# The experts' up products in wide form from the third slot on, their sums dealt among the steps of the route choice

## The chip, the core and the metric

One program runs on one core of a Trainium2 chip. The metric is the device time of one execution in microseconds (us). A core has TensorE (PE, with its weight loads shown apart as PEld), VectorE (DVE), ScalarE (ACT), GpSimd (POOL) and SyncE (SP, which here only issues transfers). The engines run side by side, each works through its own list in order, and they meet on semaphores.

## What is computed

The reference runs two transformer blocks over 256 tokens of width 1024. The change lies in the last layer of the second block, a PEER layer with 16384 experts:

```python
s1, i1 = lax.top_k(s[:, :, 0], PEER_TOPK)
s2, i2 = lax.top_k(s[:, :, 1], PEER_TOPK)
cand_s = (s1[..., :, None] + s2[..., None, :]).reshape(T, PEER_HEADS, PEER_TOPK * PEER_TOPK)
top_s, pos = lax.top_k(cand_s, PEER_TOPK)
experts = jnp.take_along_axis(cand_i, pos, axis=-1)
g = jax.nn.softmax(top_s, axis=-1).astype(xb.dtype)
act = jax.nn.gelu(jnp.einsum('td,thkd->thk', xb, u)) * g
return jnp.einsum('thk,thkd->td', act, v)
```

Each token picks 16 experts per head by two rounds of top-16 (the route choice); its output is the gated sum of those experts. Every number is fp32.

## The kernel before

The kernel does not gather rows of the expert tables. It computes gelu(u·x) for all 16384 experts, multiplies it by a gate that is zero for experts not chosen, and multiplies by the whole second table. So both tables, 64 slots of 1 MB each, stream through the core once.

**The weight stream.** SP loads the stream in halves of 512 KB (128 partitions of 1024 fp32) into a ring of 6 places (line 1398). A place is loaded again when TensorE has finished with its last content (semaphore half_multiplied). ScalarE rounds each half to the part `ring_hi` (line 1856, `split`), and GpSimd subtracts to get the rest `ring_lo` (line 1413). The operand x has been split likewise into `h_hi` and `h_lo`, which lie side by side as `h_both`. A product in fp32 quality is hi·hi + hi·lo + lo·hi.

**Narrow up products** (`channels`, called by `experts(s)`, slots 0 to 24 of the up table). For each of 8 steps over the width and each half, three matmuls of 256 columns add to one bank: `ring_hi` on `h_hi`, `ring_hi` on `h_lo`, `ring_lo` on `h_hi`: 48 matmuls in a slot. Slots use three banks in turn. ScalarE's part (`activations`, line 892) is: split two halves, wait for the slot's product, apply gelu from the bank to `H`.

**Wide up products** (`wide_product`, called by `wide_experts(s)`, slots 25 to 62). `ring_hi` is multiplied on both parts of x in one matmul of 512 columns, then `ring_lo` on `h_hi` with 256: 32 matmuls in a slot. The product hi·lo lands in the second 256 columns of each bank, so somebody must add it. ScalarE copies that half of the bank to `H` (line 926), VectorE adds it to the first half in place (`columns`, line 1258), and ScalarE applies gelu one slot later (line 923). A slot takes two banks, and slots alternate between banks 0, 1 and 2, 3: TensorE may start slot s only when gelu of slot s-2 is done (h_ready). ScalarE's list for a wide slot s (`low_products`) is: split half 2s+4 of the up table; wait for the sum of slot s-1; split half 2s+5; gelu of slot s-1; wait for TensorE's slot s; copy its low products.

**The route choice on VectorE.** For each block of 128 tokens `best` runs rounds of 8 largest values, their indices and their replacement over 16 groups of 128 and then 8 groups of 256. Then come two casts (1227, 1228), four rounds of compare, multiply and reduce (1233, 1237, 1238), and a softmax whose exponential is ScalarE's (line 905, with the waits routes_shifted before and routes_exp after). TensorE transposes the result (585 to 587), ScalarE and VectorE copy it to `ROUTE` and the lookup area. VectorE has no part in the narrow slots, so the choice has it for itself; its sums begin with slot 25. After slot 31 the gates join: one-hot products per 8 tokens between the slots.

**The order** is written out by hand for each engine; there is no planner. Loops (`Fori`) stand for slots 5 to 22 on TensorE.

Of the kernel before, what the change touches and what calls it, by code (L numbers as in the profile page):

```python
# [5 lines left out]
SEQ = 256  # L6
D = 1024
TOK = 2
# [46 lines left out]
def build(nc, dram):  # L55
# [8 lines left out]
    with ctx:  # L64
# [231 lines left out]
        FIRST_WIDE = 25  # L296
# [51 lines left out]
        def pe_second(pe, weights, weights_ready, multiplied, parts, norm_transposes, wait_operand, wait_normed, token_product, out_product):  # L348
# [240 lines left out]
            last.then_inc(S["routes_transposed"], 1)  # L589
# [121 lines left out]
        def act_second(act, split, ahead, round_to, load_roots, root, norm_act):  # L711
# [186 lines left out]
            for s in range(2, 5):  # L898
                activations(s)
            with act.Fori(0, 5) as it:  # L900
                for s in range(5, 8):
                    activations(s, it)

            act.wait_ge(S["routes_shifted"], 1)
            A.activation(TV, TV, ACT.Exp).then_inc(S["routes_exp"], 1)
            act.wait_ge(S["x_stored"], 32)
            for s in range(20, 23):
                activations(s)
            act.wait_ge(S["routes_transposed"], 1)
            A.copy(ROUTE[:, 0:2, :].rearrange("p s t -> p (s t)"), ps[:, 4, :]).then_inc(S["routes_copied"], 1)  # L910

            A.mul(ROUTE[:, 2, :], ps[:, 5, 0:256], GATE_SCALE).then_inc(S["routes_copied"], 1)
            for s in range(23, FIRST_WIDE):
                activations(s)
# [13 lines left out]
            for s in range(FIRST_WIDE, 33):  # L928
                low_products(s)
# [49 lines left out]
        def dve_second(dve, step, inverse, wait_rounded, rest_of, norm_dve):  # L979
# [219 lines left out]
            def best(rows, values, indices, low=-3e38):  # L1199

                for first in (0, 8):
                    for r, v, i in zip(rows, values, indices):
                        last = V.max(v[:, first:first + 8], r)
                    step(last)
                    for r, v, i in zip(rows, values, indices):
                        last = V.max_index(i[:, first:first + 8], v[:, first:first + 8], r)
                    step(last)
                    if first == 0:
                        for r, v, i in zip(rows, values, indices):
                            last = V.match_replace(r, v[:, 0:8], r, low)  # L1210
                        step(last)

            for t in range(TOK):
                dve.wait_ge(S["sim_copied"], t + 1)
                g = range(16)
                best([SC[:, t, n, :] for n in g], [T1V[:, t, n, :] for n in g], [T1I[:, t, n, :] for n in g])
# [5 lines left out]
                best([CS[:, t, n, :] for n in g], [TV[:, 8 * t + n, :] for n in g], [TP[:, 8 * t + n, :] for n in g])  # L1222
# [4 lines left out]
            step(V.tensor_copy(PA, PAI))  # L1227
            step(V.tensor_copy(T1F, T1I))
            dve.wait_ge(S["sk_loaded"], 32)
            for t in range(TOK):  # L1230
                for side in range(2):
                    place = PA[:, side, t * 128:(t + 1) * 128].unsqueeze(2).broadcast_to([128, 128, 16])
                    step(V.tensor_tensor(EQ.rearrange("p (g a) -> p g a", a=16), place,
                                         iota[:, 0:16].unsqueeze(1).broadcast_to([128, 128, 16]), ALU.is_equal))
                    eq = EQ.rearrange("p (h k a) -> p h k a", h=8, k=16)
# [1324 lines left out]
```

## Time and profile before

| | us |
|---|---|
| median of 3 runs | 1524.72 (1524.34 to 1526.68) |
| the profiled execution | 1527.34 |
| its span in the trace | 1525.4 |
| TensorE busy in the span | 1496.1 (98%) |
| VectorE, ScalarE, GpSimd busy | 957.5, 807.1, 1190.6 |

The up slots 2 to 24 run from 775 to 908 us of the span, the first wide slots (25 to 31) from 908 to 948, and the slots with gates from there. The route choice fills VectorE from 768 to 886. An entry of the timeline is: start, duration, engine, line, operation, output and inputs; brackets give how long the engine had been idle and what released it. Matmuls overlap, so the pace of TensorE is read from start to start, not from durations.

### The profile page before, as it was taken

How to read it: one execution, taken by the hardware profiler on the slowest of the kernel's cores; microseconds unless marked ns; L12 is line 12 of the kernel's file. 1: busy time of each engine (PE TensorE's matmuls, PEld its weight loads, DVE VectorE, ACT ScalarE, POOL GpSimd, SP SyncE). 2: the span in 40 equal slices, each digit the busy share in tenths (PEclk: the TensorE clock that was granted, in tenths of full speed). 3: DMA queues.
4: the chain of work that ended last, by engine and by line, in shares of the span. 5: the costliest groups of instructions: out<-in, count | busy, mean ns of one | idle time of the engine just before them, and what ended most of it. 6: DMA issues, size and time to landing. Idle time of an engine off the chain costs nothing.

```text
span 1525.4 us, 28491 instructions
## 1 busy us (share of the span) xinstructions
PE 1496.1 (98%) x10230; PEld 1305.8 (86%) x10230; DVE 957.5 (63%) x1382; ACT 807.1 (53%) x1091; POOL 1190.6 (78%) x501
## 2 busy tenths in 40 slices
PE   6999999999999999999999999999999999999998
PEld 5698888887899989998899998888888778788886
DVE  6654665565432578542589922877779999944444
ACT  4566655557564565545554455555554444444443
POOL 6745688885888866498978998777777777789995
PEclk9999999999999999999999999999999999999999
DMA  8624565565655543356645555555555555566663
GB/s 291 235 94 143 169 192 185 188 191 158 189 180 164 167 140 114 109 196 213 214 152 181 180 180 178 170 172 167 167 173 171 166 174 171 176 224 196 190 194 119
DMA packets 72487, 268.17 MB, mean 176 GB/s; under 512 B 8144, under 2 KB 8416, under 8 KB 71008
## 3 DMA queue, kind: packets, MB, share of 16 engines
q1 hardware_dynamic: 69696, 251.90, 52.1%
q0 software_dynamic: 1856, 9.49, 1.6%
q10 hardware_dynamic: 864, 5.77, 1.0%
q8 instruction: 53, 0.87, 0.2%
q14 instruction: 18, 0.15, 0.0%
HBM read 263.98 MB, written 3.15 MB: 175 GB/s over the span
## 4 chain that ended last, share of the span: by engine, by line
PE 59%; POOL 18%; issue 15%; DVE 5%; ACT 1%; DMA 1%; DVEq 0%; POOLq 0%; ACTq 0%; SPq 0%
PE ps L1339 58%; POOL ring_lo L1413 17%; DVE onehots_i L1267 1%; DVE h_both L2114 1%; DVE big L1286 1%; DMA ring<-in_stream 1%; DVE onehot_j L1271 1%; ACT ring_hi L1856 1%; DMA big<-in_filt 0%; DVE big L2140 0%; DVE big L2142 0%; DVE big L2139 0%; DVE h_both L2131 0%; PE ps L1588 0%; PE ps L1488 0%
## 5 line engine op out<-in xcount | busy, mean ns | idle before, releaser
L1413 POOL TENSOR_TENSOR ring_lo<-ring,ring_hi 128x1024 fp32r<-128x1024 f32 x472 | 1167.8, 2489 | 311.5 <-ACT ring_hi L1856 309.2
L1856 ACT CAST ring_hi<-ring 128x1024 fp32r<-128x1024 f32 x472 | 491.8, 1051 | 436.5 <-DMA ring<-in_stream 433.7
L1339 PE MATMUL ps<-h_both,ring_hi 128*128 128x256 f32 (+1 forms) x2816 | 703.4, 330 | 2.1 <-DVE h_both L2131 1.8
L1339 PE MATMUL ps<-h_both,ring_lo 128*128 128x256 f32 x1952 | 549.8, 282 | 0.0
L1339 PEld LDWEIGHTS ps<-h_both,ring_hi 128*128 128x128 f32 x2816 | 473.6, 190 | 54.6 <-issue 3.1
L1339 PE MATMUL ps<-ring_hi,h_both 128*128 128x512 f32 (+1 forms) x1408 | 428.9, 382 | 9.0 <-POOL ring_lo L1413 5.2
L1339 PEld LDWEIGHTS ps<-h_both,ring_lo 128*128 128x128 f32 x1952 | 371.1, 190 | 0.4
L1339 PEld LDWEIGHTS ps<-ring_hi,h_both 128*128 128x128 f32 x1408 | 259.8, 188 | 64.9 <-issue 11.0
L1339 PE MATMUL ps<-ring_lo,h_both 128*128 128x512 f32 (+1 forms) x704 | 265.5, 377 | 0.0
L2114 DVE TENSOR_TENSOR h_both<-big,h_both 128x512 fp32r<-128x512 f32 (+1 forms) x66 | 138.0, 2091 | 99.8 <-ACT h_both L1869 99.7
L1339 PEld LDWEIGHTS ps<-ring_lo,h_both 128*128 128x128 f32 x704 | 132.7, 188 | 22.6
L1339 PE MATMUL ps<-big 128*64 128x64 f32 (+11 forms) x980 | 98.7, 289 | 10.4 <-DMA big<-in_filt 8.2
L1339 PEld LDWEIGHTS ps<-big 128*64 128x64 f32 (+4 forms) x980 | 74.9, 163 | 27.8 <-issue 15.8
L1286 DVE TENSOR_TENSOR big<-ps,big 128x512 f32 (+1 forms) x64 | 86.0, 1344 | 1.5 <-ACT big L923 1.1
L1267 DVE TENSOR_TENSOR onehots_i<-routes,ps 128x1024 f16<-128x1024 f32 (+1 forms) x64 | 77.5, 1211 | 0.0
L1258 DVE TENSOR_TENSOR ps<-ps,big 128x512 f32<-128x512 f32 x38 | 26.6, 699 | 75.9 <-ACT big L926 75.9
L2376 DVE SCALAR_TENSOR_TENSOR big<-ps,vecs,big 128x255 f32<-128x255 f32 (+1 forms) x88 | 36.4, 475 | 25.8 <-ACT big L2068 25.8
L1339 PE MATMUL ps<-q_both,ring_hi 128*128 128x512 f32 x128 | 45.0, 396 | 0.0
L2381 DVE TENSOR_TENSOR ps<-big 128x256 f32<-128x256 f32 x22 | 42.3, 1923 | 3.4 <-ACT big L2044 1.2
L1869 ACT ACTIVATE h_both<-big 128x512 fp32r (+2 forms) x66 | 42.1, 640 | 3.4 <-DVE big L1286 3.3
L1271 DVE TENSOR_TENSOR onehot_j<-routes,ps 128x512 f16<-128x512 f32 (+1 forms) x64 | 43.4, 678 | 0.0
L1275 DVE TENSOR_TENSOR onehots_j_even<-onehot_j,ps 128x1024 f16<-128x1024 f16 x32 | 39.1, 1221 | 4.4
(325 smaller groups left out, 1459.6 us busy)
## 6 DMA issues: line engine op xcount, KB each, us to landing
ring<-in_stream SPq DMA_DIRECT2D x476, 512.0 KB, 3.8
big<-in_cmp_values POOLq DMA_DIRECT2D x2, 1024.0 KB, 11.5
residual<-big ACTq DMA_DIRECT2D x2, 1024.0 KB, 4.8
big<-residual ACTq DMA_DIRECT2D x2, 1024.0 KB, 6.6
x<-in_x SPq DMA_DIRECT2D x2, 512.0 KB, 5.4
big<-in_fdecay POOLq DMA_DIRECT2D x1, 1024.0 KB, 8.9
aux<-in_tab POOLq DMA_DIRECT2D x1, 1024.0 KB, 11.9
big<-in_w POOLq DMA_DIRECT2D x1, 1024.0 KB, 15.1
```

The source lines that it names most:

```text
L1258: V.tensor_tensor(sums, sums, H[:, bass.ds(at(2 * s, 12, it), 2), :], ALU.add).then_inc(S["columns_summed"], 1)
L1267: V.tensor_tensor(OA[:, q % 2], first.unsqueeze(2).broadcast_to([128, 8, 128]), IOTA.unsqueeze(1).broadcast_to([128, 8, 128]), ALU.is_equal)
L1271: V.tensor_tensor(ONEHOT_J[:, :, :], second.unsqueeze(2).broadcast_to([128, 8, 64]), IOTA[:, 64 * half:64 * half + 64].unsqueeze(1).broadc ...
L1275: V.tensor_tensor(OB[q % 2][:, :, :, :], ONEHOT_J[:, :, :].unsqueeze(1).broadcast_to([128, 2, 8, 64]), GATE_PARTS[:, :, bass.ds(tok, 8)].u ...
L1286: V.tensor_tensor(h, ps[:, bank, :].rearrange("p (t j) -> p t j", t=8), h, ALU.mult).then_inc(S["gated"], 1)
L1339: return nc.tensor.matmul(out, lhsT, rhs, start=start, stop=stop, skip_group_check=True)
L1413: P.tensor_tensor(ring_lo[:, h % RING, :], ring[:, h % RING, :], ring_hi[:, h % RING, :].bitcast(fp32), ALU.subtract).then_inc(S["split_lo ...
L1856: A.copy(ring_hi[:, h % RING, :], ring[:, h % RING, :]).then_inc(S["split_hi"], 1)
L1869: A.activation(dst, src, ACT.Copy, scale=scale).then_inc(S["operand_hi"], 1)
L2114: V.tensor_tensor(lo, src, hi.bitcast(fp32), ALU.subtract).then_inc(S["operand_lo"], 1)
L2376: V.scalar_tensor_tensor(y, ffn_place(i, j)[:, 0:SEQ - s], vecs[:, bass.ds(col, 1)], y, ALU.mult, ALU.add).then_inc(S["ffn_tap"] if tap el ...
L2381: V.tensor_tensor(gated, CONV[:, i % 2, 0, :], CONV[:, i % 2, 1, :], ALU.mult).then_inc(S["ffn_product"], 1)
```

## The change

`FIRST_WIDE` goes from 25 to 2: slots 2 to 24 take the wide form too, with all that belongs to it on ScalarE and VectorE. VectorE's 23 new sums of these slots are put between the steps of the route choice by hand (`columns_after`), and 3 more (25 to 27) after it. TensorE's transposes of the routes move from behind slot 22 to behind slot 27. On ScalarE the exponential moves from in front of slot 20 to behind the low products of slot 25, and the copies of the routes to behind those of slot 27.

```diff
-        FIRST_WIDE = 25
+        FIRST_WIDE = 2
@@ TensorE
-            for s in range(2, 5):
-                experts(s)
-            with pe.Fori(0, 6) as it:
-                for s in range(5, 8):
-                    experts(s, it)
+            for s in range(FIRST_WIDE, 5):
+                wide_experts(s)
+            with pe.Fori(0, 3) as it:
+                for s in range(5, 11):
+                    wide_experts(s, it)
+            for s in range(23, 28):
+                wide_experts(s)
...
-            for s in range(23, FIRST_WIDE):
-                experts(s)
-            for s in range(FIRST_WIDE, 32):
+            for s in range(28, 32):
                 wide_experts(s)
@@ ScalarE
+            for s in range(FIRST_WIDE, 5):
+                low_products(s)
+            with act.Fori(0, 3) as it:
+                for s in range(5, 11):
+                    low_products(s, it)
+            act.wait_ge(S["x_stored"], 32)
+            for s in range(23, 26):
+                low_products(s)
+            act.wait_ge(S["routes_shifted"], 1)
+            A.activation(TV, TV, ACT.Exp).then_inc(S["routes_exp"], 1)
+            for s in range(26, 28):
+                low_products(s)
+            act.wait_ge(S["routes_transposed"], 1)
+            A.copy(ROUTE[:, 0:2, :].rearrange("p s t -> p (s t)"), ps[:, 4, :]).then_inc(S["routes_copied"], 1)
+            A.mul(ROUTE[:, 2, :], ps[:, 5, 0:256], GATE_SCALE).then_inc(S["routes_copied"], 1)
+            for s in range(28, 33):
                 low_products(s)
@@ VectorE
                     for r, v, i in zip(rows, values, indices):
                         last = V.max(v[:, first:first + 8], r)
                     step(last)
+                    if ("max", first) in columns_after:
+                        next_columns()
...
+                     (("max", 8), ("index", 8)) + ((("index", 0), "replace") if t else ()))
...
+                     (("max", 0), "replace", ("max", 8)) if t else (("max", 0), ("index", 0), ("max", 8), ("index", 8)))
...
             step(V.tensor_copy(PA, PAI))
+            next_columns()
             step(V.tensor_copy(T1F, T1I))
+            next_columns()
...
                     step(V.tensor_tensor(EQ.rearrange("p (g a) -> p g a", a=16), place,
                                          iota[:, 0:16].unsqueeze(1).broadcast_to([128, 128, 16]), ALU.is_equal))
+                    next_columns()
...
                     step(V.tensor_reduce(IX[:, side, t, :], EQ.rearrange("p (g a) -> p g a", a=16), AX, ALU.add))
+                    next_columns()
...
             V.tensor_tensor(TV, TV, wide(inv), ALU.mult).then_inc(S["routes_ready"], 1)
+            for s in range(summed[0], 28):
+                columns(s)
```

## Rows read from the trace of the kernel before

**Rows 1.** The page, part 1: engine, busy us and share, count.

```profile
PE 1496.1 (98%) x10230; PEld 1305.8 (86%) x10230; DVE 957.5 (63%) x1382; ACT 807.1 (53%) x1091; POOL 1190.6 (78%) x501
```

**Rows 2.** The chain that ended last, 740 to 960 us: start, us, what.

```profile
739.78 156.24 PE ps L1339 x1264
...
936.79 4.43 DMA ring<-in_stream
...
942.89 17.17 PE ps L1339 x121
```

**Rows 3.** PE's timeline: narrow steps, the first wide slot, a query step.

```profile
907.90 0.28 PE L1339 MATMUL ps<-h_both,ring_lo 128*128 128x256 f32 x1
908.02 0.40 PE L1339 MATMUL ps<-h_both,ring_hi 128*128 128x512 f32 x1
...
911.91 0.40 PE L1339 MATMUL ps<-h_both,ring_hi 128*128 128x512 f32 x1
...
724.71 0.40 PE L1339 MATMUL ps<-q_both,ring_hi 128*128 128x512 f32 x1
...
730.95 0.40 PE L1339 MATMUL ps<-q_both,ring_hi 128*128 128x512 f32 x1
```

**Rows 4.** ACT's timeline beside narrow slots: gelu (L892), two splits (L1856).

```profile
792.38 0.60 ACT L892 ACTIVATE big<-ps 128x512 f32<-128x512 f32 x1 [0.96 <-PE ps L1339]
...
796.70 1.05 ACT L1856 CAST ring_hi<-ring 128x1024 fp32r<-128x1024 f32 x1 [2.09 <-DMA ring<-in_stream]
...
867.36 0.60 ACT L892 ACTIVATE big<-ps 128x512 f32 x1 [0.87 <-PE ps L1339]
...
870.90 1.05 ACT L1856 CAST ring_hi<-ring 128x1024 fp32r<-128x1024 f32 x1 [1.52 <-DMA ring<-in_stream]
```

**Rows 5.** ACT's timeline beside wide slots: copy (L926), splits, gelu (L923).

```profile
930.80 0.59 ACT L926 COPY big<-ps 128x512 f32<-128x512 f32 x1 [0.15 <-PE ps L1339]
...
935.25 1.05 ACT L1856 CAST ring_hi<-ring 128x1024 fp32r<-128x1024 f32 x1 [2.02 <-DMA ring<-in_stream]
936.21 0.59 ACT L923 ACTIVATE big<-ps 128x512 f32<-128x512 f32 x1
```

**Rows 6.** PE's timeline at a wide slot's start: idle before, releaser.

```profile
936.34 0.28 PE L1339 MATMUL ps<-h_both,ring_lo 128*128 128x256 f32 x1
936.85 0.50 PE L1339 MATMUL ps<-h_both,ring_hi 128*128 128x512 f32 x1 [0.23 <-ACT big L923]
```

**Rows 7.** DVE's timeline: the sum of a wide slot.

```profile
931.42 0.70 DVE L1258 TENSOR_TENSOR ps<-ps,big 128x512 f32<-128x512 f32 x1 [4.92 <-ACT big L926]
```

**Rows 8.** DVE's timeline: first operation of steps of the route choice.

```profile
767.79 3.19 DVE L1203 MAX8 aux<-big 128x8 f32<-128x128 f32 x16 [10.01 <-ACT big L882]
771.01 0.09 DVE L1206 MATCH_VALUE_LOAD aux<-aux,big 128x8 f32 x1
...
775.32 0.09 DVE L1210 MATCH_VALUE_LOAD big<-aux,big 128x8 f32 x1
...
855.98 4.47 DVE L1233 TENSOR_TENSOR ps<-aux 128x2048 f32<-128x2048 f32 x1
```

**Rows 9.** ACT's timeline about the exponential: table load and activation.

```profile
879.50 1.28 ACT L905 ACT_TABLE_LOAD   x1
884.11 0.42 ACT L905 ACTIVATE aux<-aux 128x256 f32<-128x256 f32 x1 [3.33 <-DVE aux L1243]
```

**Rows 10.** DVE's timeline behind the exponential.

```profile
884.56 0.42 DVE L1245 TENSOR_REDUCE stat<-aux 128x16 f32<-128x256 f32 x1 [0.49 <-ACT aux L905]
...
885.30 0.42 DVE L1247 TENSOR_TENSOR aux<-aux,stat 128x256 f32<-128x256 f32 x1
```

**Rows 11.** Busy time by stretch: engines in page order, clock, DMA share, GB/s.

```profile
775.00:896.00 121.00, 121.00 (x1011) 121.00 (x1010) 108.90 (x362) 60.42 (x66) 107.74 (x41) 1.00 0.56 177
```

**Rows 12.** GpSimd's group of 849 to 884 us, and of 885 to 907.

```profile
L1413 POOL TENSOR_TENSOR ring_lo<-ring,ring_hi 128x1024 fp32r<-128x1024 f32 x11 | 34.3, 3155 | 0.4 <-ACT ring_hi L1856 0.4
...
L1413 POOL TENSOR_TENSOR ring_lo<-ring,ring_hi 128x1024 fp32r<-128x1024 f32 x9 | 21.4, 2404 | 2.2 <-ACT ring_hi L1856 2.2
```

More of the change, by code:

```diff
@@ L897, in act_second @@
                 similarities(t)
[L898 to L914, printed above, removed]
             def low_products(s, it=None):
@@ L926, in low_products @@
                 A.copy(H[:, bass.ds(at(2 * s, 12, it), 2), :], ps[:, wide_banks(s), SEQ:2 * SEQ]).then_inc(S["low_products_copied"], 1)
-            for s in range(FIRST_WIDE, 33):
+            for s in range(FIRST_WIDE, 5):
[14 more added lines that the diff above has]
+            for s in range(28, 33):
                 low_products(s)
@@ L1196, in dve_second, with columns, next_columns, best @@
                         rest_of(SCALED[:, c, :], h_hi[:, c, :], h_lo[:, c, :])
-            def best(rows, values, indices, low=-3e38):
+            def columns(s, it=None):
+                dve.wait_ge(S["low_products_copied"], at(EXPERT_SUMS + s - FIRST_WIDE + 1, 6, it))
+                sums = ps[:, wide_banks(s), 0:SEQ]
+                V.tensor_tensor(sums, sums, H[:, bass.ds(at(2 * s, 12, it), 2), :], ALU.add).then_inc(S["columns_summed"], 1)
+            summed = [FIRST_WIDE]
+            def next_columns():
+                columns(summed[0])
+                summed[0] += 1
+            def best(rows, values, indices, columns_after, low=-3e38):
                 for first in (0, 8):
@@ L1207, in best @@
                     step(last)
+                    if ("index", first) in columns_after:
+                        next_columns()
                     if first == 0:
@@ L1215, in dve_second @@
                 g = range(16)
-                best([SC[:, t, n, :] for n in g], [T1V[:, t, n, :] for n in g], [T1I[:, t, n, :] for n in g])
+                best([SC[:, t, n, :] for n in g], [T1V[:, t, n, :] for n in g], [T1I[:, t, n, :] for n in g],
+                     (("max", 8), ("index", 8)) + ((("index", 0), "replace") if t else ()))
                 halves = T1V[:, t].rearrange("p (h s) k -> p h s k", s=2)
@@ L1221, in dve_second @@
                 g = range(8)
-                best([CS[:, t, n, :] for n in g], [TV[:, 8 * t + n, :] for n in g], [TP[:, 8 * t + n, :] for n in g])
+                best([CS[:, t, n, :] for n in g], [TV[:, 8 * t + n, :] for n in g], [TP[:, 8 * t + n, :] for n in g],
+                     (("max", 0), "replace", ("max", 8)) if t else (("max", 0), ("index", 0), ("max", 8), ("index", 8)))
             tp = TP.rearrange("p g k -> p (g k)")
@@ L1252, in dve_second @@
             dve.wait_ge(S["gate_rest"], 1)
-            def columns(s, it=None):
-                dve.wait_ge(S["low_products_copied"], at(EXPERT_SUMS + s - FIRST_WIDE + 1, 6, it))
-                sums = ps[:, wide_banks(s), 0:SEQ]
-                V.tensor_tensor(sums, sums, H[:, bass.ds(at(2 * s, 12, it), 2), :], ALU.add).then_inc(S["columns_summed"], 1)
             def onehots(q, it=None):
@@ L1292, in rest @@
                 rest_of(flat(H[:, bass.ds(at(2 * s, 2 * span, it), 2), :]), flat(h_hi[:, place, :]), flat(h_lo[:, place, :]))
-            for s in range(FIRST_WIDE, 31):
+            for s in range(28, 31):
                 columns(s)
```

19 lines of the change are left out of this document (11 added, 8 removed).

## The prediction

> **What bounds the kernel now.** The page's first part gives TensorE 98% of the span [rows 1]. A share over the whole span says nothing of one stage, so the second view is the chain of waits over the stage that is changed. There the chain is TensorE's own matmuls without a break through the narrow slots and the first wide ones. But for the transposes of the routes it leaves TensorE only near 937 us, for a transfer of the ring, a split and TensorE again [rows 2]. The third view, busy time by stretch, says that from 775 to 896 us TensorE is busy all the time, VectorE 90%, GpSimd 89% and ScalarE 50%, at full clock [rows 11]. The stage costs what its matmuls cost, and a change shows in the time as far as TensorE's slots get shorter and nothing new holds them up. All that follows the stage hangs on the same chain, so a shift here should come through to the end.
>
> **Shorter slots.** The pace is read from start to start. Narrow: 907.90 to 908.02, so 0.12 us a matmul, and 48 of them make 5.76 [rows 3]. Wide, same operands: 908.02 to 911.91 is 11 steps of one 512 and one 256 columns, 0.3536 each, so 5.65 for 16 [rows 3]. The gain is 0.11 us in each of slots 2 to 24: 23 x 0.11 = 2.5 us off. The query products with the same shapes run faster: 724.71 to 730.95 is 18 steps, 0.3467 each, 5.55 a slot [rows 3], which would give 23 x 0.21 = 4.9. I take the first, since it has the same operand and stands next to the changed slots; the other is the bound. That the wide slot is the longer one I exclude, since these rows have it shorter at either pace.
>
> What the page of TensorE makes of this: the Trainium skill, "TensorE: Matmul & The Clock Gate", section "Back-to-back issue gap", gives an isolated matmul N/2.4 + 2.5 ns. By that the narrow step would be 3 x 109.2 = 327.5 ns and the wide one 215.8 + 109.2 = 325.0, an estimate of only 0.04 us a slot and 0.9 in all. The rows show 360 and 354 ns, so the trace does not agree in size.
>
> **The loop behind a wide slot.** What the wide form adds is a chain that the narrow one, with three banks, never had to meet. Slot s+2 needs gelu of slot s. Gelu of slot s stands on ScalarE behind the split of a half whose ring place is freed only when slot s ends. From the rows: copy of slot 28 at 930.80; its second split starts at 935.25, 4.45 later, released by the transfer; gelu at 936.21; TensorE starts slot 30 at 936.85, 1.60 after the split, having waited on that gelu [rows 5, 6]. The copy starts about 0.2 after TensorE's next slot has begun when nothing stalls, so slot s+2 may begin without loss until 5.65 - 0.2 = 5.45 after the copy. The transfer may therefore take 5.45 - 1.6 = 3.85 us from the copy to the split. In narrow slots the same distance is 3.54 (867.36 to 870.90) at best and 4.32 (792.38 to 796.70) at worst [rows 4]; these two are the ends of 21 such pairs, six of which exceed 3.85, by 0.9 us together. Of the wide slots 25 to 31 two lost 0.4 each: slot 30 could have begun 0.12 after 936.34 and began at 936.85, and slot 31 at 942.89 came 6.04 after it [rows 2, 6]. At the narrow pairs' rate 23 new slots lose about 1.0 us. If every fourth met the 4.45 of slot 28, 0.6 too much, they would lose 5.75 x 0.6 = 3.5; if every one did, half of it each, since a slot begun late gives the next one room: 6.9. The former has more samples, and I take it: +1.0, from 0 to 3.5.
>
> **The sums on VectorE.** A sum takes 0.70 and can begin 0.62 us after the copy of its low products starts (930.80 to 931.42) [rows 5, 7]. It costs nothing if done before ScalarE's second split, 3.8 us after the copy. VectorE reaches them between steps of the choice. A step of 16 maxima takes 3.2 us, one of 16 indices or replacements 4.3 [rows 8]; a compare takes up to 4.5. Between two sums there are two steps at most. Laying them out against slots of 5.65, VectorE is ahead and waits at slots 3, 5, 7, 10, 11, 12, and from 16 on at nearly each. The tightest is slot 8: from slot 7's sum, at which VectorE waited, 0.65 + 0.70 + 3.2 + 4.3 + 0.7 = 9.55 after the copy of slot 7, against 5.65 + 3.8 = 9.45. That is 0.1 late; with the next tight one, slot 13 (0.5 to spare), I take +0.2, from 0 to 1.5 if steps come out a few per cent longer. The choice, whose softmax began at 884.56 [rows 10], ends at about 907, since VectorE is now tied to TensorE's pace. TensorE wants the routes behind slot 27, about 923, and the gates' copies after slot 31, about 946, so that delay is hidden.
>
> **The exponential.** In the kernel before it cost TensorE nothing: three banks, and ScalarE waited for VectorE inside slack. Now it stands behind the low copy of slot 25, and the sum of slot 25 stands behind the softmax on VectorE. From that copy's start: copy 0.6, table load 1.28, exponential 0.42 [rows 9], VectorE's reduce to product 884.56 to 885.72, 1.2 [rows 10], sum 0.7: 4.2 us. Only then ScalarE may split the second half (not at 3.8), and ahead of gelu it must load gelu's table again, 1.28 [rows 9]: 4.25 + 1.6 + 1.3 = 7.15 after the copy, where 5.45 is free. Slot 27 is held up by +1.7 us. Without VectorE's part it would be 3.75 + 1.6 + 1.3 - 5.45 = 1.2, the lower bound; the upper is 2.5 with a late transfer. One slot later the loop has recovered: the place for the next split was freed in time, and slot 27 itself takes 5.65.
>
> **Costs at nothing.** GpSimd needs 2.4 us a half when alone and took 3.16 in the compare steps [rows 12]. Those steps cost it some 8 us beyond 11 x 2.4, whatever the pace; 46 halves x 2.4 plus that and 3 more for casts are 121 of 130 us. It can lag some 6 us before TensorE waits, since a half is needed 13.8 us after its place is freed and takes 3.8 + 1.05 + 2.4. The copies (0.6 a slot) fall on ScalarE's idle half. Six transposes move and cost the same 0.7. SP's queue keeps its order; its loads come 2% closer together. Slots 2 and 3 meet no wait, since gelu of slots 0 and 1 is long done.
>
> **Sum.** -2.5 + 1.0 + 0.2 + 1.7 = +0.4 us, on the profiled execution's 1527.34 (span 1525.4 and 1.9 around it). That execution lies 2.6 above the median of the runs, so I put the same +0.4 on the median: 1525.1.
>
> **The rivals.** *The query pace.* The new slots run at 5.55, the free time drops to 5.35, and stalls eat a little more (1.3): -4.9 + 1.3 + 0.2 + 1.7 = -1.7, 1523.0; with no stall on transfers and the short form of the exponential -3.7, 1521.0. For it: two measured levels and no row that names the cause; against it: all wide slots on `h_both` here stand at 5.65. Chance 0.22. *The transfer becomes the bound,* the case on the slow side: beyond 3.85 us between copy and split it costs time. With slot 28's 4.45 in every fourth slot: -2.5 + 3.5 + 0.2 + 1.7 = +2.9, 1527.6; with it in all, -2.5 + 6.9 + 1.9 = +6.3, 1531.0. For it: the only stretch of this form without gates ended in such stalls, and the chain shows it [rows 2]; against it: the distances of the narrow slots, whose transfers come only 2% less often [rows 4]. Chance 0.17. *VectorE late:* if the steps with interleaved sums run 5% longer, slots 4, 8, 9 and 13 come late by up to 0.5 each: +2.4, 1527.1. Chance 0.03. *The slot does not get shorter:* 5.76 as before, with room of 3.96 for the transfer: 0 + 0.5 + 0 + 1.6 = +2.1, 1526.8. It would do so if the 512 columns cost what two matmuls of 256 cost; the row at 908.02 speaks against it. The page named above comes near this, with 0.04 a slot. Chance 0.05. *The forecast,* between -2 and +2.5: 0.53.
>
> **How the numbers follow.** A run of this kernel can tell about 0.2%, 3 us, from no change. The forecast's case holds 0.47 of "same" and 0.03 on either side; the query pace 0.10 same and 0.12 faster; the transfer 0.05 same and 0.12 slower; the two small ones 0.05 same and 0.03 slower. Faster 0.15, same 0.67, slower 0.18. The range runs from the low end of the query pace, 1521.2, to 1529.0, well into the transfer's case, and leaves out about 1 in 8.
>
> **What would show it.** In the profile after: starts of slots 5.65 apart (step 0.354) in slots 3 to 24; TensorE idle 0.1 to 0.5 us before a few slots with gelu (the activation of `low_products`) as releaser; one stall of 1.7 before slot 27 with two table loads beside it; VectorE idle before most sums from slot 16 on; 23 more sums of 0.70 us. A step of 0.347 in those slots, distances from copy to split above 4 as a rule, or GpSimd as TensorE's releaser would make the prediction wrong.

## The result: slower by 0.3%

| | before | after |
|---|---|---|
| median in us (8 runs each) | 1526.66 (1524.34 to 1527.74) | 1531.48 (1527.87 to 1533.41) |
| the profiled execution, us | 1527.34 | 1528.75 |
| its span | 1525.4 | 1526.9 |
| slots 2 to 25, start to start | 133.2 | 133.3 |
| slots 25 to 31, start to start | 34.9 | 36.4 |

The ratio of the times is 1.0032 (95% interval 1.0021 to 1.0043). The last two rows of the table are read from the starts of the slots' first matmuls; the six transposes of the routes (0.66 us) lie in the first of them before and in the second after. The prediction was +0.4 us, so 1525.1, in a range from 1521.2 to 1529.0; the change costs 4.8 us here, and 1531.48 lies above the range. 2 us of the distance to 1525.1 are the kernel before itself, which measured 1526.66 in these runs and not 1524.72; even without them it would be 1529.5.

The page of the kernel after, part 1, answers [rows 1]:

```profile
PE 1494.1 (98%) x9862; PEld 1285.5 (84%) x9862; DVE 962.6 (63%) x1405; ACT 818.2 (54%) x1114; POOL 1187.3 (78%) x501
```

368 matmuls are gone (23 slots x 16), TensorE is busy 2 us less, and the span is 1.5 us longer: the work got shorter and the waits ate more than that. Busy time by stretch, 775 to 908 us, of the kernel after, with the columns of [rows 11]:

```profile
775.00:908.00 133.00, 131.39 (x736) 112.00 (x735) 112.07 (x375) 73.68 (x92) 117.09 (x46) 1.00 0.53 177
```

TensorE, which was busy without a break in the narrow slots [rows 11], now idles 1.6 us in this stretch alone, and GpSimd, at 117 of 133 us (88%, against 89% before), is no closer to being the bound. The chain that ended last shows where the breaks come from (start, us, what; kernel after). It answers [rows 2], but the pattern now stands in the choice's stretch:

```profile
739.94 51.59 PE ps L1358 x347
791.55 0.04 SPq L1417
791.69 3.95 DMA ring<-in_stream
795.72 0.09 ACT ring_hi L1875
...
796.68 0.59 ACT big L906
797.27 0.23 issue
797.50 23.18 PE ps L1358 x128
```

A ring place is freed at 791.55, the transfer takes 3.95 us, the split and gelu follow, and slot 6 begins only then. ScalarE's and TensorE's timelines at the same place (kernel after; L909 is the copy of low products, L1875 the split, L906 gelu) answer [rows 5] and [rows 6]:

```profile
791.56 0.59 ACT L909 COPY big<-ps 128x512 f32<-128x512 f32 x1 [0.52 <-PE ps L1358]
...
795.72 1.05 ACT L1875 CAST ring_hi<-ring 128x1024 fp32r<-128x1024 f32 x1 [1.83 <-DMA ring<-in_stream]
796.68 0.59 ACT L906 ACTIVATE big<-ps 128x512 f32 x1
```

```profile
797.50 0.47 PE L1358 MATMUL ps<-h_both,ring_hi 128*128 128x512 f32 x1 [0.34 <-ACT big L906]
```

From copy to second split it is 4.16 here, and from the split to TensorE's start 797.50 - 795.72 = 1.78. In the slots written out without a loop it had been 1.60 [rows 5, 6].

The stall before slot 27, from the same chain (L920 is the exponential and its table load, L1201 the sum of slot 25 behind the softmax, L906 gelu's table load):

```profile
913.56 0.59 ACT big L909
...
914.16 1.28 ACT L920
...
915.46 0.43 ACT aux L920
...
917.07 0.62 DVE ps L1201
...
917.72 1.05 ACT ring_hi L1875
...
918.79 1.28 ACT L906
...
920.73 5.92 PE ps L1358 x32
```

920.73 - 913.56 = 7.17 from the copy, where the prediction had 7.15.

### The profile page after: what moved, and what is told of

It is laid out like the page before. It is cut to its first block, busy times and chain, and to the rows that moved or that the text cites. A ratio compares the mean times of both kernels' runs of the same rounds, so it can differ in the third digit from the quotient of the medians.

```text
span 1526.9 us, 27863 instructions
## 1 busy us (share of the span) xinstructions
PE 1494.1 (98%) x9862; PEld 1285.5 (84%) x9862; DVE 962.6 (63%) x1405; ACT 818.2 (54%) x1114; POOL 1187.3 (78%) x501
## 4 chain that ended last, share of the span: by engine, by line
PE 59%; POOL 18%; issue 15%; DVE 3%; DMA 3%; ACT 2%; POOLq 0%; DVEq 0%; SPq 0%; ACTq 0%
PE ps L1358 58%; POOL ring_lo L1432 17%; DMA ring<-in_stream 2%; ACT ring_hi L1875 1%; DVE onehots_i L1286 1%; DMA big<-in_filt 0%; DVE h_both L2133 0%; ACT big L906 0%; DVE big L2159 0%; DVE big L2161 0%; DVE big L2158 0%; DVE onehot_j L1290 0%; DVE h_both L2150 0%; DVE big L1305 0%; PE ps L1607 0%
## 5 line engine op out<-in xcount | busy, mean ns | idle before, releaser
L1875 ACT CAST ring_hi<-ring 128x1024 fp32r<-128x1024 f32 x472 | 492.1, 1051 | 442.1 <-DMA ring<-in_stream 435.9
L1358 PE MATMUL ps<-h_both,ring_hi 128*128 128x512 f32 (+1 forms) x2448 | 699.8, 353 | 5.4 <-ACT big L906 3.1
L1358 PEld LDWEIGHTS ps<-h_both,ring_hi 128*128 128x128 f32 x2448 | 427.9, 189 | 76.4 <-issue 7.6
L1358 PEld LDWEIGHTS ps<-ring_lo,h_both 128*128 128x128 f32 x704 | 132.6, 188 | 22.5
L1201 DVE TENSOR_TENSOR ps<-ps,big 128x512 f32<-128x512 f32 x61 | 42.7, 699 | 78.7 <-ACT big L909 78.4
L909 ACT COPY big<-ps 128x512 f32 (+1 forms) x61 | 35.8, 587 | 40.4 <-PE ps L1358 40.2
L2395 DVE SCALAR_TENSOR_TENSOR big<-ps,vecs,big 128x255 f32<-128x255 f32 (+1 forms) x88 | 36.4, 475 | 25.6 <-ACT big L2087 25.6
```

Source lines behind the costliest of these rows:

```text
L909: A.copy(H[:, bass.ds(at(2 * s, 12, it), 2), :], ps[:, wide_banks(s), SEQ:2 * SEQ]).then_inc(S["low_products_copied"], 1)
L1201: V.tensor_tensor(sums, sums, H[:, bass.ds(at(2 * s, 12, it), 2), :], ALU.add).then_inc(S["columns_summed"], 1)
L1358: return nc.tensor.matmul(out, lhsT, rhs, start=start, stop=stop, skip_group_check=True)
L1875: A.copy(ring_hi[:, h % RING, :], ring[:, h % RING, :]).then_inc(S["split_hi"], 1)
L2395: V.scalar_tensor_tensor(y, ffn_place(i, j)[:, 0:SEQ - s], vecs[:, bass.ds(col, 1)], y, ALU.mult, ALU.add).then_inc(S["ffn_tap"] if tap el ...
```

## The experiments

A table of what the profiles show comes first, since the texts below use it. "2 to 25" and the others are distances between the starts of those slots; the ratio is to runs of the kernel before on the same chip. In the kernels whose name begins with "before" slots 2 to 24 are narrow. The six transposes (0.66) lie in 2 to 25 there, and in 25 to 31 elsewhere; in before_late_transposes they lie in 25 to 31 too.

| kernel | 2 to 25 | 25 to 31 | gated, 34 to 58 | ratio (95% interval) |
|---|---|---|---|---|
| before | 133.2 | 34.9 | 149.1 | |
| before_again | 133.2 | 34.4 | 149.1 | 1.0003 (0.9993 to 1.0013) |
| before_third | 133.2 | 34.3 | 146.8 | |
| after | 133.3 | 36.4 | 149.1 | 1.0032 (1.0021 to 1.0043) |
| after_again | 133.6 | 36.6 | 149.1 | 1.003 (1.002 to 1.004) |
| after_third | 132.8 | 36.8 | 149.1 | |
| exp_as_copy | 132.7 | 35.8 | 146.7 | 1.0016 (1.0005 to 1.0026) |
| unrolled | 133.5 | 37.0 | 149.1 | 1.0027 (1.0013 to 1.004) |
| unrolled_gelu_first | 127.7 | 35.2 | 146.7 | 0.9961 (0.9945 to 0.9976) |
| loops_gelu_first | 130.0 | 35.1 | 146.7 | 0.9969 (0.9957 to 0.9981) |
| exp_in_gap | 129.6 | 34.3 | 146.7 | 0.9962 (0.9948 to 0.9975) |
| sums_earlier | 129.7 | 34.3 | 146.7 | 0.9973 (0.996 to 0.9986) |
| sum_behind_pairs | 127.7 | 34.2 | 149.4 | 0.9959 (0.9944 to 0.9974) |
| before_gelu_first | 133.6 | 33.9 | 149.1 | 1.0011 (1.0002 to 1.002) |
| before_late_transposes | 133.1 | 34.3 | 146.7 | 0.9986 (0.9977 to 0.9995) |
| gelu_first_from_28 | 132.6 | 36.1 | 146.7 | 1.0018 (1.0007 to 1.0028) |

Three theories stood at the start. A: the loop from a freed place over transfer, split and gelu sets the start of a wide slot. B: VectorE's sums, squeezed between the steps of the choice, come late. D: something outside slots 2 to 31 differs from one execution to the next. A fourth, E, came up on the way.

### The changed kernel again

after_again, no edit.

> The changed kernel once more, unedited, for a second profile: its times fell into two groups, near 1528 (the profiled one) and near 1532. If the distance from the copy of low products to the second split sets the start of wide slots (theory A), the total of TensorE's idle time before the slots 2 to 31 accounts for all that one execution has over another: an execution of 1532 shows some 4 us more in starts of slots 4 to 31 than the 1528 one, and those slots show distances above 3.9. If something outside the stage varies (theory D), the starts of slots 2 to 31 are the same in both and the difference lies before 774 or behind 950 us. Median against before: 1.003.

Its median is 1527.75 on a chip where the kernel before has 1523.2, so the change costs about the same there, 4.6 us. Its profiled execution took 1527.61, 1.1 us less than the first one, and yet more in the stage: 170.3 us from slot 2 to 31 against 169.8. So what separates these two executions lies outside the stage, as theory D has it. No profile caught an execution near 1532, and what those do otherwise stays open.

The second profile also shows a wait that the first has not. ScalarE's second split behind the copy of slot 4 is released by VectorE's sum and not by the transfer (L909 copy, L1875 split, L1201 the sum):

```profile
792.40 0.58 ACT L909 COPY big<-ps 128x512 f32<-128x512 f32 x1 [0.51 <-PE ps L1358]
793.49 1.05 ACT L1875 CAST ring_hi<-ring 128x1024 fp32r<-128x1024 f32 x1 [0.51 <-DMA ring<-in_stream]
796.72 1.05 ACT L1875 CAST ring_hi<-ring 128x1024 fp32r<-128x1024 f32 x1 [2.17 <-DVE ps L1201]
```

TensorE idles 0.55 us before slot 6 for it. The third profile has the same wait, 4.27 us from copy to split. Theory B therefore holds for one slot in two of three profiles; TensorE's other waits for gelu between slots 4 and 25 stand behind a transfer.

### The exponential left out

```diff
-            A.activation(TV, TV, ACT.Exp).then_inc(S["routes_exp"], 1)
+            A.activation(TV, TV, ACT.Copy).then_inc(S["routes_exp"], 1)
```

> The exponential of the routes' softmax is left out (a copy stands in its place), so ScalarE loads no other table in the stage. All other waits stay. If the two table loads are what holds slot 27 (1.6 us in the profile of the changed kernel), slot 27 starts 5.7 after slot 26 and the time falls by 1.6 (ratio to before 1.002 instead of 1.003). If VectorE's place behind the softmax is what holds it, less than 0.4 us is gained.

The ratio fell from 1.003 to 1.0016, about 2 us (1.4 by the medians), with intervals that overlap. In the profile slot 27 started 6.34 after slot 26 and not 7.4: a transfer took 4.86 from copy to split just there, so a good part of the stall stayed under another name. Without the table loads the stall is smaller in this profile, which supports the step; the exact 1.6 isn't shown by this run. Its gated slots ran 2.4 us faster (34 to 58), which was not expected and could by itself account for the gain in the median. It is what led to the last theory below.

### Without the loops

```diff
-            with pe.Fori(0, 3) as it:
-                for s in range(5, 11):
-                    wide_experts(s, it)
+            for s in range(5, 23):
+                wide_experts(s)
```

and the same for `low_products` on ScalarE.

> Slots 5 to 22 written out without the loops on TensorE and ScalarE, same order. In the changed kernel's loops TensorE starts a slot 1.78 after the second split, against 1.60 in the slots written out. Theory A: that 0.18 falls on most of 18 slots, so the mean start-to-start there goes from 5.80 to 5.68 and the time falls by about 2 us, somewhat less as stalls share. Theory B (VectorE's sums come late): no change in the mean, 5.80. If the instruction fetch of the longer programs disturbs the transfers, it gets slower instead, with more distances above 4.2.

The expected 2 us did not come: the ratio stayed at 1.0027, and 2 to 25 took 133.5. The first eleven slots were as theory A had them, 5.69 on the mean against 5.79 in the kernel after. Then came transfers of 4.74, 5.21 and 4.35 us from copy to split, with slots of 6.30, 6.77 and 6.15. Here is the worst, ScalarE's timeline of this kernel (L908 copy, L1873 split, L905 gelu):

```profile
865.62 0.59 ACT L908 COPY big<-ps 128x512 f32<-128x512 f32 x1
866.67 1.05 ACT L1873 CAST ring_hi<-ring 128x1024 fp32r<-128x1024 f32 x1 [0.46 <-DMA ring<-in_stream]
870.83 1.05 ACT L1873 CAST ring_hi<-ring 128x1024 fp32r<-128x1024 f32 x1 [3.10 <-DMA ring<-in_stream]
871.78 0.59 ACT L905 ACTIVATE big<-ps 128x512 f32<-128x512 f32 x1
```

The instruction queue of this kernel moved 8 pieces in the stage against 5 in the kernel after. That these disturb the stream is not shown; after_again, with its loops, had a transfer of 4.77 too. What is shown is that TensorE pays for every long transfer, loop or not.

### Gelu ahead of the second split

```diff
                 if s > FIRST_WIDE:
                     act.wait_ge(S["columns_summed"], at(EXPERT_SUMS + s - FIRST_WIDE, 6, it))
-                split(2 * n + 5, it, 6)
+                if s >= 33:
+                    split(2 * n + 5, it, 6)
                 if s > FIRST_WIDE:
                     A.activation(H[:, bass.ds(at(2 * s - 2, 12, it), 2), :], ps[:, wide_banks(s - 1), 0:SEQ],
                                  ACT.Gelu_apprx_tanh).then_inc(S["h_ready"], 1)
+                if s < 33:
+                    split(2 * n + 5, it, 6)
```

on top of the kernel without loops.

> As the one without loops, and in ScalarE's list gelu of slot s-1 stands ahead of the second split up to slot 32, so that TensorE's next slot no longer waits for a transfer. Theory A: TensorE starts every slot from 4 on without a wait, 5.65 apart (only slot 27 is held by the softmax, some 1.0 instead of 1.6); against the unrolled one another 1.5 to 2, in all 4 below the changed kernel and at or 1 us below the kernel before. Theory B: the stalls stay, now with gelu waiting for VectorE's sum, and nothing is gained.

This one edit is worth 10 us by the ratios (0.9961 where it had been 1.0027) and 11.6 by the medians, 1516.98 against 1528.53, beside 1523.2 of the kernel before. Expected were 1.5 to 2 against the unrolled kernel. In the two profiles 7.7 us of it lie in slots 2 to 31 and 3.1 behind them, in the gated slots, to which the last theory comes back. Slots 3 to 25 ran at 5.54 to 5.55, faster than the 5.65 expected. ScalarE's timeline (L911 copy, L906 gelu, L1876 split):

```profile
873.77 0.57 ACT L911 COPY big<-ps 128x512 f32<-128x512 f32 x1
875.39 1.06 ACT L1876 CAST ring_hi<-ring 128x1024 fp32r<-128x1024 f32 x1 [1.05 <-DMA ring<-in_stream]
876.35 0.59 ACT L906 ACTIVATE big<-ps 128x512 f32<-128x512 f32 x1
878.22 1.05 ACT L1876 CAST ring_hi<-ring 128x1024 fp32r<-128x1024 f32 x1 [1.27 <-DMA ring<-in_stream]
```

The second split begins 4.45 after the copy, as late as at slot 28 of the kernel before, and the median over this kernel's slots is 4.37 against 3.82 in the kernel after. The transfers got slower, TensorE does not notice, because gelu is done by 876.9 and the next slot needs it at 879. Theory A holds: with the transfer out of the way of gelu the stalls of slots 4 to 26 are gone, though the sums come in the same order. Luck has a small part in it: the sum of slot 4 was in time in this profile, as in that of the unrolled kernel, and late in most others (see the pair sums below).

### The same with the loops kept

The edit above on the kernel after, with a copy of one column between wait and gelu.

> The changed kernel with its loops, and gelu ahead of the second split up to slot 32 (behind a copy of one column that costs 0.2 us of ScalarE). Theory A: as without the loops: slots 2 to 25 in 127.7 us (5.55 each), median 10 below the changed kernel, ratio to before 0.996. If writing out the loops was part of that gain, it stops short, at 5.65 or above and a ratio of 0.998.

Ratio 0.9969, so the loops are not what cost most of the time. But 2 to 25 took 130.0, not 127.7: slots 3 and 4 ran at 5.55 (5.63 for slot 2), slots 5 and 6 took 5.78 and 5.73 because the sum of slot 4 came late, and every slot behind them ran at 5.65 with no wait in front. The same shape showed up in the next run.

### The exponential in the gap

```diff
+                if s == 26:
+                    act.wait_ge(S["routes_shifted"], 1)
+                    A.activation(TV, TV, ACT.Exp).then_inc(S["routes_exp"], 1)
                 if s < 33:
                     split(2 * n + 5, it, 6)
```

and on VectorE the sum of slot 25 ahead of the wait for routes_exp.

> No loops, gelu first, and the exponential stands between gelu and second split of slot 26, with the sum of slot 25 ahead of VectorE's wait for it, so its two table loads fall where ScalarE waits for a transfer. Slot 27 starts 5.55 after slot 26 instead of 6.54: 1.0 us below unrolled_gelu_first, ratio to before 0.9955. If the table loads hold up gelu of slot 26 instead, slot 28 takes what slot 27 gives, and nothing is gained.

Slot 27 started 5.65 after slot 26, and slot 28 gave nothing back: the softmax's stall of 1 us is gone, as expected. The ratio is 0.9962 all the same, since 2 to 25 took 129.6. The cause stands in three timelines of this kernel. VectorE (L1201 the sum, L1214 the 16 maxima of the second block), ScalarE, TensorE:

```profile
810.25 0.70 DVE L1201 TENSOR_TENSOR ps<-ps,big 128x512 f32<-128x512 f32 x1
810.86 3.18 DVE L1214 MAX8 aux<-big 128x8 f32<-128x128 f32 x16
818.39 0.70 DVE L1201 TENSOR_TENSOR ps<-ps,big 128x512 f32<-128x512 f32 x1
```

```profile
814.19 0.59 ACT L914 COPY big<-ps 128x512 f32<-128x512 f32 x1 [0.75 <-PE ps L1359]
815.19 1.05 ACT L1876 CAST ring_hi<-ring 128x1024 fp32r<-128x1024 f32 x1 [0.41 <-DMA ring<-in_stream]
819.12 0.60 ACT L906 ACTIVATE big<-ps 128x512 f32<-128x512 f32 x1 [2.88 <-DVE ps L1201]
```

```profile
819.42 0.28 PE L1359 MATMUL ps<-h_both,ring_lo 128*128 128x256 f32 x1
819.77 0.50 PE L1359 MATMUL ps<-h_both,ring_hi 128*128 128x512 f32 x1
```

The sum of slot 8, the one that the prediction called the tightest, is done 4.9 after its copy; gelu waits for it, and slot 10 starts at 819.77 and not at 819.53. The stall is 0.24 us. But up to there a 512- and a 256-column matmul together had a step of 0.3467, and from the slot at 819.77 to the transposes all had 0.3533. A wait of a quarter of a microsecond cost 0.1 in each of 17 slots behind it.

### Sums one step earlier

sums_earlier puts one more sum behind the first 16 maxima of the second block, and the last one among its 8 groups behind the last indices; sum_behind_pairs besides puts the sum of slot 4 right behind the pair sums of the first block.

```diff
-                     (("max", 8), ("index", 8)) + ((("index", 0), "replace") if t else ()))
+                     (("max", 8), ("index", 8)) + ((("max", 0), ("index", 0), "replace") if t else ()))
```

> exp_in_gap with the order of VectorE changed in the second block of tokens: a sum also behind the first 16 maxima, and the last of the 8-group sums behind the last indices. In exp_in_gap the sum of slot 8 came at 818.4, 4.2 after its copy; gelu waited, slot 10 started 0.24 late, and from there the slots ran at 5.65 to slot 27. If so, now slots 3 to 27 run at 5.55, start of slot 31 less start of slot 2 is 161.6 instead of 163.9, and the time is 1.5 to 2 us below exp_in_gap. If the step is chance, it falls anywhere between.

> sums_earlier with the sum of slot 4 right behind the pair sums of the first block of tokens (one step earlier), since there it came 5.1 after its copy and slot 6 started late. If late sums are what turns the step, slots 3 to 27 stay at 5.55 and slot 2 to slot 31 takes 161.6 (164.0 in sums_earlier), median near 1516 on a chip where the kernel before has 1523.5, ratio 0.9955. If a slot turns to 5.65 without a late sum or another wait before it, the step is chance.

sums_earlier missed: 164.0 from slot 2 to 31. Now slot 4's sum was the late one (second split 5.13 after the copy), slot 6 took 5.69, and from there all ran at 5.65. The pair sums in front of it took 4.5 us; here are GpSimd and VectorE in sum_behind_pairs, L1434 the subtraction of a half, L1236 the pair sums:

```profile
788.51 2.43 POOL L1434 TENSOR_TENSOR ring_lo<-ring,ring_hi 128x1024 fp32r<-128x1024 f32 x1 [0.29 <-ACT ring_hi L1877]
788.56 4.53 DVE L1236 TENSOR_TENSOR big<-aux 128x2048 f32<-128x2048 f32 x1
793.12 0.70 DVE L1201 TENSOR_TENSOR ps<-ps,big 128x512 f32<-128x512 f32 x1
```

In the first profile of the kernel after the pair sums of the first block started together with GpSimd's subtraction:

```profile
787.91 4.54 POOL L1432 TENSOR_TENSOR ring_lo<-ring,ring_hi 128x1024 fp32r<-128x1024 f32 x1 [0.37 <-ACT ring_hi L1875]
787.91 2.28 DVE L1236 TENSOR_TENSOR big<-aux 128x2048 f32<-128x2048 f32 x1
```

There GpSimd took 4.54 and VectorE 2.28. Of the eleven profiles with wide slots from slot 2 on three show it so; in the other eight, after_again and after_third among them, GpSimd started 0.04 to 0.17 us earlier, took 2.4, and the pair sums took 4.4 to 4.5. (In the kernel before they took 3.1, with GpSimd 1.4 ahead.) The Trainium skill, "SBUF — State Buffer", section "Who interferes with whom", says that a VectorE instruction with both inputs in SBUF contends with one of GpSimd that reads SBUF, and that the order of issue decides who is held up; the traces agree, and the one held up loses 2.1 to 2.3 us. So whether the sum of slot 4 was late in the kernel after was a draw of each execution.

With that sum moved, sum_behind_pairs had 127.7 from slot 2 to 25, with the pair sums at 4.53, and 162.0 to slot 31 (161.6 expected). It is the change as it could have been: ratio 0.9959, median 1517.24 against 1522.64, even though its profiled execution had the slow step in the gated slots. The differences among the five kernels with gelu first from slot 3 on are within their intervals; that each of them beats the kernel before is not.

### What the step costs behind the stage

Theory E came from these profiles: TensorE runs the wide product at one of two steps, and keeps it until an interruption. The gated slots of two profiles of one and the same kernel, TensorE's timeline, first before_third and then before_again (each the first wide matmul behind a gate's products):

```profile
1047.99 0.47 PE L1339 MATMUL ps<-h_both,ring_hi 128*128 128x512 f32 x1
...
1054.10 0.47 PE L1339 MATMUL ps<-h_both,ring_hi 128*128 128x512 f32 x1
```

```profile
1048.43 0.48 PE L1339 MATMUL ps<-h_both,ring_hi 128*128 128x512 f32 x1
...
1054.64 0.48 PE L1339 MATMUL ps<-h_both,ring_hi 128*128 128x512 f32 x1
```

6.11 us a slot in the one, 6.21 in the other, at the same granted clock (1.00 from 962 to 1112 us in both). Over 31 slots that is 3 us that no edit made.

> The kernel before once more, unedited, for a second profile. The wide products run at one of two steps, 0.3533 or 0.3467 us, and keep it until something interrupts them; the 31 gated slots behind (0.1 us each) were at the slow one in the first profile of the kernel before (slots 34 to 58 in 149.1 us, against 146.7). Theory E: which step the gated slots get is chance in each execution, and this alone moves a run by some 3 us. Then this profile shows either 149.1 or 146.7, and its time lies 3 us lower with the latter. Rival: the kernel before always has 149.1. Ratio 1.000.

> The kernel before for one more profile: 149.1 or 146.7 from slot 34 to 58. Theory E allows either, with a time some 3 us lower with 146.7; its times reach from 1520.6 to 1527.7, and both profiles so far (149.1) stand in the upper half.

> The changed kernel for one more profile: its gated slots at 149.1 (slots 34 to 58) and 170 from slot 2 to 31, as in the two profiles before, if stalls decide how it enters the gated slots; 146.7 if that is an even chance.

The kernel before had 149.1 twice and 146.8 once; the profiled executions took 1527.34 and 1526.04 with the first and 1524.19 with the second. The kernel after had 149.1 three times. The level that slot 31 ends with is also that of slots 34 to 58 in 13 of the 16 profiles; it turned at slots 32 to 34 in before_third and exp_as_copy (slow to fast) and in after (fast to slow).

```diff
             for s in range(FIRST_WIDE, 28):
                 wide_experts(s)
+            routes_transposes()
             for s in range(28, 32):
                 wide_experts(s)
```

before_late_transposes: in the kernel before with gelu first for slots 25 to 32, the transposes and the copies that follow them move behind slot 27.

> The kernel before with one edit: gelu ahead of the second split for slots 25 to 32. Theory A: the stalls before slots 29 to 31 (0.07, 0.4, 0.4) go, start of slot 31 less start of slot 25 falls from 34.9 to 33.9 at the slow step or 33.3 at the fast one, time 1 us lower (ratio 0.999). This is what the order alone is worth without the wide form in slots 2 to 24, so that the rest of the 6 us below the kernel before belongs to the two together.

> The kernel before with gelu first for slots 25 to 32 and, as in the changed kernel, the six transposes of the routes behind slot 27 instead of 22 (with their copies); slots 2 to 24 stay narrow. In five profiles the first slot behind these transposes ran 5.64 and the next, if not held up, 5.55 a slot. Theory E (TensorE keeps one of two steps until an interruption picks again): slots 29 to 31 and the 31 gated slots run at the fast step, slots 34 to 58 take 146.7 instead of 149.1, and the time is 3.5 us below before_gelu_first (ratio to before 0.998). If the gated step is chance in every execution, the median stays at before_gelu_first's and the runs scatter over 3 us.

before_gelu_first did what it should in its slots (25 to 31 in 33.9), and yet came out at 1.0011 and not at 0.999. Its profile also has a wait of some 0.4 us for GpSimd's part of a half before slot 22, which the edit does not touch; before_late_transposes has one like it (hence 133.1 from slot 2 to 25). Slot 25, the first wide one, ran at the slow step here as in all five profiles with narrow slots before it, and with no stall behind it TensorE went into the gated slots at that step; its runs (1523.46 to 1526.43) lack the low end that the kernel before has on the same chip (from 1520.96). before_late_transposes, with the same work in another order, entered them fast: 146.7, and 1521.34 against 1524.89, 3.55 us less where 3.5 was expected. The two ran on different chips, on which the kernel before has 1523.58 and 1523.4; the ratios, 0.9986 and 1.0011, say the same, and their intervals are apart. So the step is not chance in each slot; the transposes gave a fast one, and it lasted. The edit also moves ScalarE's and VectorE's copies, but the two profiles differ by 0.2 us from slot 2 to 31 and by 3.1 from slot 31 to 62. The transposes do not always give it: of twelve profiles with them behind slot 27, ten had slot 28 at the fast step, exp_as_copy and sum_behind_pairs at the slow one.

> The changed kernel with gelu ahead of the second split in slots 28 to 32 alone. Slots 2 to 27 stay as they are. If the stalls of slots 29 to 31 decide the step of the gated slots, these slots now run at 5.55, slots 34 to 58 take 146.7, and the median falls by 0.6 + 3.1 = 3.7 us, to a ratio to before of 1.0005. If the rest of the loss lies elsewhere, only 0.6 is gained and the ratio stays at 1.0025.

This is the kernel after with only the stalls of slots 29 to 31 removed. The gated slots ran at 146.7 in the profile and slots 29 and 30 at 5.55. The ratio is 1.0018 (1.0007 to 1.0028) against 1.003 (1.002 to 1.004): 1.8 us gained on the central values, between the 0.6 and the 3.7 of the two expectations, and the intervals allow either. One of its runs reached 1529.8. So this run does not settle how much of the loss the gated slots are.

## Why the prediction was wrong

**The bound** was read rightly: TensorE's chain, no release by GpSimd (in slots 2 to 31 of the three profiles of the kernel after TensorE waits for gelu alone), a shift that comes through to the end.

**The step that failed** is the loop behind a wide slot, put at +1.0. Take the three profiles of the kernel after from slot 2 to 25. 12 to 20 of the 46 half slots (8 of a slot's 16 steps each) ran at 0.3467 and the others at 0.3533; by themselves they would take 129.0 to 129.4 us, a gain of 3.1 to 3.5 over the 132.5 of the narrow slots, where the prediction had 2.5. Interruptions at the starts of slots cost the rest, 3.4 to 4.4 us, on the mean 4.0, where loop and sums together were put at 1.2.

**Shorter slots, -2.5.** Too small, in the favour of the change. The 0.3536 of the rows next to the change is not the price of the wide form on this operand; it is one of two levels, and 0.3467 was the other. With nothing in the way the 23 slots take 127.7 against 132.5 narrow, a gain of 4.9, the figure that the prediction kept as its bound. It had listed both levels and chosen by neighbourhood. Against the faster one it held that all wide slots on `h_both` in the trace before stand at 5.65, and that was misread: slot 28 has it, 14 steps in 4.85 us, 0.3464 each.

```profile
925.40 0.40 PE L1339 MATMUL ps<-h_both,ring_hi 128*128 128x512 f32 x1
...
930.25 0.40 PE L1339 MATMUL ps<-h_both,ring_hi 128*128 128x512 f32 x1
```

In the first profile of the kernel after, 28 of the 60 half slots from slot 2 to 31 ran at the fast step and 32 at the slow one. The prediction's estimate from the Trainium skill, "TensorE: Matmul & The Clock Gate", section "Back-to-back issue gap", had 325.0 ns for the pair and 327.5 for the narrow form. Both levels and the narrow 360 lie above it, and the saving of 7 to 13 ns is larger than its 2.5.

**The loop behind a wide slot, +1.0.** The mechanism was right and its size was not. From slot 2 to 25 the kernel after took 133.3, 133.6 and 132.8, on the mean 133.2; 132.5 less 2.5 plus 1.0 plus 0.2 had been 131.2, 2 us less. One part of it is a threshold taken from slots outside a loop: there 1.60 from split to TensorE's start, in the loop 1.78. So a transfer had 3.67 us and not 3.85 before TensorE waits (3.57 behind a slot at the fast step), and the measured distances of slots 2 to 24 had a median of 3.81, 3.76 and 3.74: of 69 in the three profiles 53 were over 3.67 and 19 over 3.85. How much of the 2 us that is, no run isolates: in the unrolled kernel the threshold was the better one, and three long transfers filled the gap. What is shown is that the loss goes when the transfer no longer stands before gelu. The rival "the transfer becomes the bound", given 0.17, was right in direction and in what it added, 3.5 (the mean of 133.2 is 3.3 over 23 slots of 5.65). Its reason was not: no run of transfers of 4.45 came, and distances above 4 were not the rule. And the nearness of 3.5 is in part chance, since it takes all slots at the slow step.

**The sums on VectorE, +0.2.** About right in size, with the wrong slot. In the first profile of the kernel after no sum of slots 2 to 24 held ScalarE up; in the two others that of slot 4 did, and slot 6 began 0.7 and 0.65 us late. Slot 4 was named only in the rival "VectorE late". Slot 8, named as the tight one, became a cost in exp_in_gap, once the larger waits were gone; what was not foreseen is that a stall of 0.24 us costs 1.7 more through the step.

**The exponential, +1.7.** Slot 27 started 7.28, 7.40 and 7.83 after slot 26, so 1.6 to 2.2 over 5.65; exp_in_gap removed it. So this term was right. The Trainium skill, "ScalarE: Activation LUTs", section "What ACT_TABLE_LOAD costs", gives about 1283 ns for the load and with a drain of about 1380 ns some 2.66 us for a switch to another set. The load agrees: both took 1.28 here. The drain does not show: ScalarE's next instruction began 0.02 us after the load (914.16 + 1.28 to 915.46).

**Costs at nothing.** GpSimd, the copies and the transposes cost TensorE no wait in the kernel after, as said. What was left out is the step at which the work behind the stage runs; the prediction had no term for it. From slot 2 to 31 the kernel after lost 2.2 us to the kernel before (169.9 against 167.7 on the mean of three profiles each), and the profiled executions themselves differ by 2.1. The medians differ by 4.6 to 4.8, so about half of the loss stands in no pair of profiles. The gated slots can be a part of it: they were slow in three of three profiles against two of three, and that is worth 3 us in an execution. How large that part is on the mean of many executions stays open: gelu_first_from_28 takes it between nothing and all.

## What to carry to other kernels

Before a product is made cheaper, follow the chain from the ring place that it frees to the wait in front of its own next slot: here a split that needed a transfer stood in front of a gelu that needed nothing, and swapping the two was worth 10 us, more than the 4.9 that the change itself could give; some 3 of the 10 came through the step of the slots behind. A threshold between such a chain and the slot must be measured in the same form of code, loop or not, and with the distribution of the transfer, not its mean. When two levels of a pace stand in one trace, price the change with both before choosing, look whether a slot of the same operand has the other one, and look for what interrupts TensorE where they change. Where two engines reach for the same memory within a tenth of a microsecond, one profile shows one order of the two: take a second before calling a step in time.

## What the runs showed of the hardware

- The same stream of one 512- and one 256-column matmul ran at 0.3533 or at 0.3467 us a pair, at the full clock in both cases (granted clock 1.00 in the stretches). A level held over 15 slots and more and changed only at the start of a slot, behind a wait or behind other products. The waits could be short: 0.24 us in exp_in_gap at 819.77 (fast to slow), 0.01 before slot 29 of before_again (fast to slow). Behind the narrow products slot 25 was slow in five of five profiles; behind the transposes slot 28 was fast in ten of twelve (5.73 us and slow in exp_as_copy and sum_behind_pairs). The gate's products between the gated slots left it as it was from slot 34 to 58 in all sixteen. What decides the level is not settled; an interruption can turn it either way or leave it.
- From gelu's start to the start of the slot that waited for it there are 0.64 us in slots outside a loop and 0.82 in the loop of slots 5 to 22 (936.21 to 936.85, 796.68 to 797.50). The loop by itself may not be the reason: slot 34 of before_third, in the loop of the gated slots, has 0.64.
- VectorE's pair sums (128x2048, both inputs in SBUF) and GpSimd's subtraction (128x1024) exclude each other where they meet: 2.28 and 4.54 us when they started together, 4.53 and 2.43 when GpSimd was 0.05 us ahead.
- A transfer of 512 KB of the same stream lasted, from the copy to the split that it released, 3.5 to 3.9 us as a rule and up to 5.2; with slots of 5.55 in place of 5.8 the median rose to 4.37 in one kernel (unrolled_gelu_first) and stayed at 3.8 in another (sum_behind_pairs). Why is not shown.
